# A three-block network on one core: the gates and the spatial mixing of the last stage put ahead of the latents, all its products taken in seven block products for eight

## The reference, cut to what matters

```python
proj = einsum('bsd,de->bse', h, w_in)        # 1024 x 2464: c_q 256, c_kv 128, k_rope 32, z_a 512, u 512, v 512, z_b 512
attn = causal attention over 8 heads from c_q, c_kv, k_rope                       # 2048 x 512
out_a = attn * silu(z_a)
u, v = gelu(u), layernorm(gelu(v), sgu_norm_g, sgu_norm_b)
sv = einsum('hts,bcshd->bcthd', tril(w_spatial), v in chunks of 128 tokens, 8 heads of 64) + b_spatial
out_b = u * sv * silu(z_b)
merged = concatenate([out_a, out_b], axis=-1)
h = layernorm(2 ** 0.25 * h + merged @ w_out, ln_g, ln_b)                         # w_out 1024 x 1024
```

## Time and profile before

| what | value |
|---|---|
| median of three runs | 4182.16 us |
| the profiled execution: time, span | 4184.42 us, 4182.7 us |
| TensorE busy | 3909.9 us (93%) |
| VectorE, ScalarE, GpSimd busy | 1937.2, 1348.6, 545.4 us |
| merge gates stage, from its first to the next stage's first matmul | 1772.45 to 2165.39 |
| residual stage | 2377.2 to 2619.5 |
| latents | 2619.57 to 2801.3 |
| attention | 2801.3 to 3444.8 |
| last stage | 3444.8 to 4182.7 |

### The profile page before, as it was taken

The page is one execution under the profiler, slowest core; times in us unless marked ns, Lnnn a source line. Parts: engine busy times, 40 slices in busy tenths (PEclk is TensorE's granted clock), DMA queues, the critical chain, the costliest instruction groups (busy, mean ns, idle before and its releaser), DMA issues. The chain is left out here.

```text
span 4182.7 us, 51121 instructions
## 1 busy us (share of the span) xinstructions
PE 3909.9 (93%) x19931; PEld 2068.6 (49%) x19931; DVE 1937.2 (46%) x3383; ACT 1348.6 (32%) x2592; POOL 545.4 (13%) x554
## 2 busy tenths in 40 slices
PE   6999899997899989999999898889999999999998
PEld 3444454443677754444444343335555555555554
DVE  6688337551566655112137577434344331232222
ACT  3333132552455557010100001115565551222221
POOL 0000000000666630022123321000000000000000
PEclk8999999998999999999999999899999999999999
DMA  5223482667455543223236332400000004010110
GB/s 189 48 52 54 87 180 80 138 119 140 146 166 166 169 139 116 80 81 121 90 110 210 128 115 91 123 25 3 8 7 2 6 13 164 30 45 30 35 41 25
DMA packets 585690, 373.56 MB, mean 89 GB/s; under 512 B 411667, under 2 KB 521335, under 8 KB 582531
## 3 DMA queue, kind: packets, MB, share of 16 engines
q1 hardware_dynamic: 571939, 315.57, 27.3%
q0 software_dynamic: 9184, 38.28, 2.5%
q10 hardware_dynamic: 4352, 16.78, 1.0%
HBM read 244.20 MB, written 126.36 MB: 89 GB/s over the span
## 5 line engine op out<-in xcount | busy, mean ns | idle before, releaser
L626 PE MATMUL bank<-uT,front_W 128*128 128x512 f32 (+1 forms) x1216 | 489.3, 564 | 4.7 <-ACT front_b_ L833 4.7
L558 PE MATMUL bank<-uT,front_W 128*128 128x512 f32 (+1 forms) x896 | 363.6, 564 | 0.0
L626 PEld LDWEIGHTS bank<-uT,front_W 128*128 128x128 f32 x1216 | 232.8, 192 | 252.7 <-issue 246.2
L2973 PE MATMUL bank<-out_W,out_xT 128*128 128x512 f32 x768 | 337.4, 596 | 6.1 <-DMA out_W<-in_w_in 6.1
L558 PEld LDWEIGHTS bank<-uT,front_W 128*128 128x128 f32 x896 | 170.1, 191 | 183.1 <-issue 179.8
L2726 PE MATMUL bank<-kT,attn_qT 96*128 96x512 f32 (+3 forms) x640 | 248.4, 540 | 7.4 <-ACT kT L2783 6.8
L2973 PEld LDWEIGHTS bank<-out_W,out_xT 128*128 128x128 f32 x768 | 145.4, 191 | 183.0 <-issue 183.0
L1600 PE MATMUL bank<-uT,gates_W 128*128 128x512 f32 x512 | 224.1, 596 | 8.3 <-DMA gates_W<-in_w_in 8.3
L3009 PE MATMUL bank<-uT,out_mT 128*128 128x512 f32 x512 | 224.2, 596 | 0.7 <-ACT out_mT L3032 0.7
L2805 ACT ACTIVATE attn_pT<-bank 128x512 f32<-128x512 f32 (+1 forms) x288 | 157.5, 574 | 125.1 <-PE bank L2743 123.6
L2950 POOL DMA_DIRECT2D out<-out_r x16 | 8.5, 534 | 1368.0 <-DVE out_r L3089 1324.8
(11 more groups left out here) (462 smaller groups left out, 6486.2 us busy)
## 6 DMA issues: line engine op xcount, KB each, us to landing
scan_gq<-gla_asks_keys_values SPq DMA_DIRECT2D x36, 768.0 KB, 7.5
scan_dq<-delta_qkv SPq DMA_DIRECT2D x32, 768.0 KB, 6.1
gla_asks_keys_values<-front_a SPq DMA_DIRECT2D x16, 1152.0 KB, 11.4
merge_W<-in_w_in SPq DMA_DIRECT2D x16, 1024.0 KB
merge_gates<-merge_r ACTq DMA_DIRECT2D x16, 1024.0 KB, 4.0
uT<-merge_gates SPq DMA_DIRECT2D x16, 1024.0 KB, 8.9
front_W<-in_w_in SPq DMA_DIRECT2D x28, 512.0 KB, 10.6
delta_qkv<-front_b_ SPq DMA_DIRECT2D x8, 1152.0 KB, 9.9
```

Of the source, the lines that this page charges most:

```text
L558: m = pe.matmul(bank[:, conv_bank(f, b), 0:n], W[:, f % 2, k, :], uT[:, k, t0:t0 + n], start=(k == 0), stop=(k == KT - 1))
L626: mm = pe.matmul(bank[:, b, 0:n], W[:, s, k, :], uT[:, k, t0:t0 + n], start=(k == 0), stop=(k == KT - 1))
L2973: m = pe.matmul(bank[:, n, :], xT[:, s, k, :], W[:, k, n, :], start=(k == 0), stop=(k == KT - 1))
```

## The change

- The weights of the first two z_b column blocks (1 MB) are loaded during the residual stage, into the part of `uT` behind `hT` (`extra`).
- A new phase `phase_hidden_gates` follows the residual stage. It computes silu(z_b) and silu(z_a), transposed, in 8 steps of seven products (4 pairs of 128 columns by 2 halves of 1024 tokens), and ScalarE stores them to DRAM (`z_d`). SP meanwhile loads the weights of v and u (`VW`, 4 MB).
- A new phase `phase_hidden_mix` computes v and u for 8 pairs of token tiles in seven products each (ring of 6 banks), Gelu, the norm of v, the spatial product, the turn and the gate, and GpSimd stores the transposed out_b to DRAM (`b_d`). The spatial product and the turn of pair p-1 stand between the products of pair p. The turning of w_spatial and b_spatial, which was at the start of the last stage, is behind the products of pair 0.
- The latents no longer store `shT`.
- `phase_output` keeps the gate of attention's output (`attended`, in place on `oT`), the output product in seven products a pair of tiles (ring of 8 banks) and the output norm; its loads are w_out in four quarters, silu(z_a) and out_b a pair, and the residual tiles. Its hardware loop is gone.

```diff
-def phase_residual(chip, x, smT, shared, w_loaded, gate_d, ln_g, ln_b, sh, hT):
+def phase_residual(chip, x, smT, shared, w_loaded, gate_d, ln_g, ln_b, sh, hT, extra, w_next, wz_saved):
...
+                if p == 2:
+                    sp.dma_start(extra, w_next[:, C_ZB:C_ZB + 2 * P].rearrange("(k p) n -> p k n", p=P)).then_inc(wz_saved, 16)
 
...
+def phase_hidden_gates(chip, hT, extra, w_in, wz_saved, VW, v_saved, z_d):
...
+            def weights(q):
+                if q >= 2:
+                    sp.wait_ge(T.sem, T.at(q - 2, "m4"))
+                c = PAIRS[q % HALF]
+                sp.dma_start(weights_of(q), w_in[:, c:c + 2 * P].rearrange("(k p) n -> p k n", p=P)).then_inc(w_loaded[q % 2], 16)
+            weights(1)
+            for i, j in ((0, 0), (1, 0), (0, 1), (1, 1)):
+                k, c = slice(i * H, (i + 1) * H), (C_V, C_U)[j]
+                sp.dma_start(VW[:, k, j * BANK:(j + 1) * BANK],
+                             w_in[:, c:c + BANK].rearrange("(k p) n -> p k n", p=P)[:, k, :]).then_inc(v_saved[2 * i + j], 16)
+            for q in range(2, STEPS):
+                weights(q)
+
...
+            for q in range(STEPS):
+                g, s, w = q // HALF, q % 2, weights_of(q)
...
+                product("m1", w[:, LO, 0:P], u(0, 0))
+                product("m2", w[:, HI, 0:P], u(1, 0))
+                pe.wait_ge(G.sem, G.at(q, "s4"))
+                pe.wait_ge(DT.sem, DT.at(g, "t2"))
+                product("m6", S[:, s, 1], t(2))
+                pe.wait_ge(DT.sem, DT.at(g, "t3"))
+                product("m7", w[:, LO, P:2 * P], t(3))
+                product("m5", S[:, s, 0], t(1))
+                product("m3", S[:, s, 2], u(1, 1))
+                pe.wait_ge(DT.sem, DT.at(g, "t4"))
+                product("m4", w[:, HI, P:2 * P], t(4))
...
+                    act.activation(r[:, s, n, :], r[:, s, n, :], ACT.Silu).then_inc(AS(f"silu{n}"), 1)
+                act.wait_ge(AS.sem, AS.at(q, "silu1"))
+                act.dma_start(z_d[2 * j:2 * j + 2, :, g * PAIR:(g + 1) * PAIR].rearrange("n p t -> p n t"), r[:, s]
+                              ).then_inc(stored[s], 16)
...
+            def sums(g):
+                u11, u12, u21, u22 = (hT[:, h, tokens(g, n)] for h in (LO, HI) for n in range(2))
+                if g:
+                    dve.wait_ge(T.sem, T.at(HALF - 1, "m5"))
+                dve.tensor_tensor(TU[:, 0], u12, u11, ALU.subtract).then_inc(DT("t1"), 1)
+                dve.wait_ge(DT.sem, DT.at(g, "t1"))
+                dve.tensor_tensor(TU[:, 1], u22, TU[:, 0], ALU.subtract).then_inc(DT("t2"), 1)
+                dve.tensor_tensor(TU[:, 2], u22, u12, ALU.subtract).then_inc(DT("t3"), 1)
+
+            def last_sum(g):
+                if g:
+                    dve.wait_ge(T.sem, T.at(HALF - 1, "m4"))
+                dve.wait_ge(DT.sem, DT.at(g, "t2"))
...
+                if q == HALF - 1:
+                    sums(1)
+                dve.wait_ge(T.sem, T.at(q, "m3"))
...
+def phase_hidden_mix(chip, hT, extra, VW, v_saved, z_d, sgu_g, sgu_b, w_spatial, b_spatial, b_d):
...
+            sums(0)
+            for w in (1, 3):
+                pool.wait_ge(v_saved[w], 16)
+            pool.wait_ge(DW.sem, DW.at(0, "t1"))
+            pool.tensor_tensor(T3, W22, W12, ALU.subtract).then_inc(GW("t3"), 1)
+            sums(1)
...
+            def product(p, name, left, right):
+                i = 7 * p + PRODUCTS.index(name) - 6
...
+            def spatial(p, e):
+                pe.wait_ge(DN[e].sem, DN[e].at(p, "vn"))
+                if e:
+                    pe.wait_ge(DX.sem, DX.at(p, "sv0"))
+                elif p:
+                    pe.wait_ge(DX.sem, DX.at(p - 1, "b1"))
+                else:
+                    pe.wait_ge(prep, 3)
+                for h in range(AH):
+                    mm = pe.matmul(bank[:, 6, h * DV:(h + 1) * DV], wsT[:, h, :], vu[:, p % 2, e, 0, h * DV:(h + 1) * DV],
+                                   start=True, stop=True)
+                mm.then_inc(TX(f"spatial{e}"), 1)
+
+            def turn(p, e):
+                pe.wait_ge(DX.sem, DX.at(p, f"su{e}"))
+                for f in range(F):
+                    tr = pe.transpose(bank[:, 7 - e, f * P:(f + 1) * P], vu[:, p % 2, e, 1, f * P:(f + 1) * P], chip.ident[:])
+                tr.then_inc(TX(f"turned{e}"), 1)
+
...
+                product(p, "m1", tile_of(p, 0, LO), W11)
+                if p == 0:
+                    pe.wait_ge(v_saved[2], 16)
+                product(p, "m2", tile_of(p, 0, HI), W21)
+                if p:
+                    spatial(p - 1, 0)
+                else:
+                    pe.wait_ge(DW.sem, DW.at(0, "t2"))
+                pe.wait_ge(G.sem, G.at(p, "s4"))
+                product(p, "m6", S[:, s, 1], T2)
+                if p == 0:
+                    pe.wait_ge(GW.sem, GW.at(0, "t3"))
+                product(p, "m7", S[:, s, 2], T3)
+                if p:
+                    spatial(p - 1, 1)
+                product(p, "m5", S[:, s, 0], T1)
+                if p:
+                    turn(p - 1, 0)
+                product(p, "m3", S[:, s, 3], W22)
+                if p:
+                    turn(p - 1, 1)
+                else:
+                    pe.wait_ge(DW.sem, DW.at(0, "t4"))
+                product(p, "m4", tile_of(p, 1, HI), T4)
+                if p == 0:
+                    pe.wait_ge(once, 32)
+                    pe.wait_ge(prep, 1)
+                    pe.transpose(bank[:, 7, 0:AH], bs[:], chip.ident[0:AH, 0:AH]).then_inc(prep_pe, 1)
+                    pe.wait_ge(prep, 2)
+                    for h in range(AH):
+                        tr = pe.transpose(bank[:, 6 + h // 4, (h % 4) * P:(h % 4 + 1) * P], ws[:, h, :], chip.ident[:])
+                    tr.then_inc(prep_pe, 1)
...
+            for p in range(NP):
+                keep(p)
+                gelu(p, "v0", "c11")
+                if p:
+                    root(p - 1, 1)
+                gelu(p, "u1", "c22")
+                gelu(p, "u0", "c12")
+                root(p, 0)
+                gelu(p, "v1", "c21")
...
+            def mix(p, e):
+                v, u = vu[:, p % 2, e, 0, :], vu[:, p % 2, e, 1, :]
+                dve.wait_ge(TX.sem, TX.at(p, f"spatial{e}"))
+                dve.tensor_tensor(by_head(v), by_head(bank[:, 6, :]), bcast(bsT[:], 2, DV), ALU.add).then_inc(DX(f"sv{e}"), 1)
+                dve.wait_ge(DX.sem, DX.at(p, f"sv{e}"))
+                dve.wait_ge(AG.sem, AG.at(p, "u0"))
+                dve.tensor_tensor(u, u, v, ALU.mult).then_inc(DX(f"su{e}"), 1)
...
+                v0, u0, v1, u1 = (vu[:, s, e, n, :] for e in range(2) for n in range(2))
+                if p >= 2:
+                    dve.wait_ge(TX.sem, TX.at(p - 2, "turned1"))
+                dve.wait_ge(A.sem, A.at(p, "s1"))
+                dve.wait_ge(T.sem, T.at(p, "m2"))
+                dve.tensor_tensor(v0, x("m2"), kept[:], ALU.add).then_inc(DC("c11"), 1)
...
+                dve.wait_ge(T.sem, T.at(p, "m3"))
+                dve.wait_ge(DC.sem, DC.at(p, "c22"))
+                dve.tensor_tensor(u0, x("m3"), u0, ALU.add).then_inc(DC("c12"), 1)
+                if p == 0:
+                    dve.wait_ge(once, 32)
+                    dve.tensor_tensor(ws, ws, bcast(chip.low[:], 1, AH), ALU.mult).then_inc(prep, 1)
+                    dve.wait_ge(rows_loaded, 32)
+                norm(p, 0)
+                if p:
+                    gated(p - 1, 1)
+                dve.wait_ge(T.sem, T.at(p, "m4"))
+                dve.tensor_tensor(v1, x("m4"), v1, ALU.add).then_inc(DC("c21"), 1)
+                if p == 0:
+                    dve.wait_ge(prep_pe, 1)
+                    dve.tensor_copy(bsT[:], bank[:, 7, 0:AH]).then_inc(prep, 1)
+                    dve.wait_ge(prep_pe, 2)
+                    for n in range(2):
+                        c = dve.tensor_copy(wsT[:, 4 * n:4 * n + 4, :], bank[:, 6 + n, :].rearrange("p (h c) -> p h c", h=4))
+                    c.then_inc(prep, 1)
...
-            with sp.Fori(0, QT) as t:
-                sp.dma_start(shT[bass.ds(t, 1)].rearrange("a p (k c) -> (a p) k c", k=KT),
-                             hT[:, :, bass.ds(t * P, P)]).then_inc(shT_stored, 16)
...
+            def pair(p):
+                s, c = p % 2, slice(2 * p * P, 2 * (p + 1) * P)
+                if p >= 2:
+                    sp.wait_ge(T.sem, T.at(p - 2, "m4"))
+                    sp.wait_ge(G.sem, G.at(p - 2, "s4"))
+                sp.dma_start(za[:, s], z_d[F:2 * F, :, c].rearrange("f p t -> p f t")).then_inc(m_loaded[s], 16)
+                sp.dma_start(b_[:, s], b_d[:, :, c].rearrange("f p t -> p f t")).then_inc(m_loaded[s], 16)
...
+            def sums(p):
+                s = p % 2
+                pool.wait_ge(DA.sem, DA.at(p, "a"))
+                if p >= 2:
+                    pool.wait_ge(T.sem, T.at(p - 2, "m3"))
...
+
+            sums(0)
+            for w in (1, 3):
+                pool.wait_ge(w_loaded[w], 16)
```

(58 more changed lines are left out.)

615 lines of the change are left out of this document (426 added, 189 removed).

## The result

The changed kernel takes 4128.4 us (median; 4126.2 to 4130.4), the one before 4181.6 (4179.4 to 4183.9) in runs on the same chip: ratio 0.987, 95% interval 0.986 to 0.989. That is 53 us less, where 64 were forecast; 4128.4 lies in the range (4106 to 4136) and 10 us above the predicted 4118.

The account below looks back on a forecast made before the run. TensorE's matmul columns were taken to bound the kernel: gates 201.5, mixing 247.5 and output 224.4 sum to 673.4 us against 737.8, 64.4 less than the 4182.2 median, so 4118 us; range 4106 to 4136, about 8 in 10.

Parts of the forecast that it names:

- the bounds on the borders: Error ranges of the stage starts, ends and waits: 2 + 3 + 4 + 5 us each way, not all at once.
- the output tail: End of the output stage: two norms, the store and the last product's way to its sum, 19.6 us.
- the redone sums: Gates stage, step 3: half the token sums are made again while TensorE has other products; counted as nothing.
- The start of the gates: First products of the gates stage: 1.8 us for the lower clock plus a 1 us stall (0 to 3).
- The start of the mixing stage: First products of the mixing stage: 1.8 us for the lower clock plus 1 us waiting for GpSimd's T3.
- The end of pair 0: Mixing stage: TensorE waits for VectorE's copy of turned b_spatial behind a norm; 4.3 us with 8 transposes (0 to 8).
- Mixing tail: Serial end of the mixing stage: last sum, Gelu, norm, passes, spatial product, turn, store and border; 18 us (14 to 24).
- Seven mixing pairs: Mixing stage: 24.04 us of products plus 4.3 of spatial products and turns a pair, 28.4, with VectorE's 27.5 under that.
- Output, pair 0: Start of the output stage: m6 starts near 19 us after loads, pair 0 done at 36.5 (32 to 44).
- that rival's time: GpSimd and VectorE slow each other in output and mixing pairs: 10 to 20 us over 15 pairs, 4128 to 4138; 12%.
- The late load: Rival, output pairs: a load over about 8 us costs one for one in up to six pairs; 4190 at 20; 2%.
- The other two: Rivals: borders hide more, 10 us back, 4100 to 4108 (7%); a wait repeats in mixing, 4 us in seven pairs, 4146 (5%).

## Why the prediction was right, and where it was short

The gain is the one that was forecast, less 10.9 us, and the errors all point one way: no term came out clearly too large. That the time still lies in the range, at the upper end of the sum's own 4108 to 4129, is due to the bounds on the borders, not to errors that cancel.

**What bounds the stage** was right: columns of matmul are time. Steps are 24.03 us in the gates and output stages and the eighth product costs its 3.43 us.

**The terms that held**: the gates' end border (6.4; last sum 2811.82 to 2818.14, 6.3), latents and attention (825), VectorE and its norms under TensorE's pace, the loads, the output tail (19.6), no cost for the redone sums, shT at nothing, ScalarE's table loads at 1.28 us without a drain.

**The terms that were too small**, 10.9 us in all:

- The start of the gates (1.8 for the clock, 1 for the stall): m6 11.1 us after m1 for 6.9, so 4.3 for 2.8. Clock and stall were added as two terms; in fact the start waits for GpSimd's fourth sum, and whatever the clock costs before it is hidden under that wait. What was mis-sized is GpSimd's chain: the forecast saw that all its sums would lie beside VectorE's and put that at 1 us without working it out, and three of them took 2 us longer each. The rest of the stage took 0.1 more than told.
- The start of the mixing stage (1.8 and 1): m5 starts 19.1 us after m1 where four products are 13.7, 5.4 for 2.8. I had reckoned GpSimd's T3 as the only late thing, and not its four sums beside T1, T2 and T4. The row that shows it was in my hands, with the stall told for the gates and forgotten here.
- The end of pair 0 (4.3, bounds 0 to 8): 6.7, and 0.8 more at a lower clock behind it. The wait is the one that I named; 2.1 of the 2.4 extra are, by the lengths of the passes and not by a run of its own, the mask pass and two passes of the norm beside GpSimd's sums (1.79, 1.09 and 1.63 for 1.2, 0.55 and 0.69).
- Mixing tail (18): 19.3, a chain of VectorE (busy for 9.5 of it), Gelu, roots and spatial products. The last spatial product and the turn take 3.65 and 1.11 us, at a granted clock of 0.50, the lower of the two levels (1.2 GHz); I had put 3.0 for both, though 4.3 was my own figure for that level.
- Seven mixing pairs of 28.48 instead of 28.34: 1.0. Each of the two products behind a spatial product takes 3.49 us instead of 3.43.
- Output, pair 0 (36.5): 37.6. The wait for T3, which stands behind T2, is 0.7 of it. The rest is no more than this start varies: 36.7 to 38.7 us in the seven profiled executions with the same loads and code there.

So the sum failed not in what bounds the stage but in the size of its border terms. The largest part, some 6 of the 10.9 us, is contention of GpSimd and VectorE in first pairs: 1.5 and 2.6 at the two starts, where holding VectorE's sums gave back 2.0 and 2.3, and 2.1 at the end of pair 0. The lower clock makes another 0.8 behind that pause and the 1.3 of the tail. I had the contention as 1 us at the start of the gates and as a rival for the pairs, where TensorE covers it, and not as a term of every border, where nothing does.

**The rivals.** GpSimd and VectorE do slow each other, but in the pairs it costs nothing (21.9 under 24.05), so that rival's time (4128 to 4138) was just met for another reason. The late load's price was wrong: I took a wait ahead of VectorE's work as TensorE's wait. A consumer that may lag behind gives its lag back only at the end. Between 6.9 and 17.2 us of delay the price, by the rows behind pair 0, goes from 0.5 to 16.5 us, not from 26 to 88. The other two did not occur.

## What to carry to other kernels

Price borders as carefully as the loop: in the loop the bounding engine covers contention, late loads and norms, and at each stage's start and end nothing does; here 62 us were forecast for borders, 73 were measured (684.3 less 576.9 of products and 34.7 of spatial products and turns), and 12 could be won back without touching a loop. Work that is needed once (turning a weight) goes between products where another engine is idle, not behind the first round. When two engines both sum SBUF tiles before the first product needs them, decide their order by who is needed first, and make the other's passes short or late. And before a delay is priced one for one, ask how far its consumer may lag: the ring's depth says it, and so does what else the consumer makes for the next product (here oT, for GpSimd's sums); the lag is paid in the tail.

## What the runs showed of the hardware

- GpSimd and VectorE passes over SBUF exclude each other by whole instructions, and the profile counts the wait as busy time: 3.2 to 3.3 us for a 1.27 us sum beside passes of 2.29, 2.1 to 2.25 beside passes of half that length, 6.55 for a T3 of 4.5 that was issued 0.1 us too late, 6.40 for a T4 of 2.29 behind it. Passes of VectorE that read a bank took their 0.68 to 0.69 us beside such sums too (3926.56 in the changed kernel, beside GpSimd's sum at 3926.12).
- After a pause of 4.6 us the granted clock of TensorE fell when it went on: 0.55 from 2852.5 to 2856.2 us, near the lower of its two levels (1.2 GHz), and 1.00 from 2856.2 on, so that the two products behind the turning took 7.83 us for 7.03. In six other executions with the same pause they took 7.66 to 8.52.
- The stages ahead of the change ended at 2612.8 to 2619.6 us in the thirteen executions that were profiled, whatever stands behind them. A difference of spans under 7 us says nothing; the length of a stage is steadier. Where the code and loads are the same, the gates stage is 203.1 us in seven kernels, latents and attention are 825.1 to 825.9 in nine (823.7 and 826.5 in two that load a quarter of W_out there), the mixing stage is 255.5 to 256.4 in five and the output stage, whose start waits for loads, 224.5 to 225.8 in five. So a difference of one us in the last two says nothing either.
